# Norms with a token on each partition, a root taken ahead of the wait, and tiles that start at whole lines

## The reference, cut to what matters

```
def rmsnorm(x, g):
    xf = x.astype(jnp.float32)
    y = xf * lax.rsqrt(jnp.mean(xf * xf, axis=-1, keepdims=True) + NORM_EPS)
    return (y * g.astype(jnp.float32)).astype(x.dtype)
...
h = rmsnorm(x, norm_mlp_g[i])
x = x + jnp.square(jax.nn.relu(h @ mlp_w1[i].astype(dt))) @ mlp_w2[i].astype(dt)
```

## Time and profile before

| | |
|---|---|
| median of 3 runs | 3005.48 us |
| profiled execution | 3006.16 us |
| its span | 3004.8 us |
| mean granted clock of PE | 0.946 |
| PE busy | 2687.6 us, 89% |
| PEld busy | 2184.9 us, 73% |
| DVE busy | 1499.9 us, 50% |
| ACT busy | 948.8 us, 32% |
| POOL busy | 173.7 us, 6% |
| DMA, mean over the span | 88 GB/s |

### The profile page before, as it was taken

One profiled execution on the slowest core, in us unless ns is written; L12 is line 12 of the kernel. 1 busy time (PEld: TensorE's weight loads), 2 busy tenths in 40 slices (PEclk: granted clock), 3 DMA queues, 4 the chain that ended last, 5 costly groups with the idle time before them and its releaser, 6 DMA issues.

```text
span 3004.8 us, 33501 instructions
## 1 busy us (share of the span) xinstructions
PE 2687.6 (89%) x14472; PEld 2184.9 (73%) x14472; DVE 1499.9 (50%) x1836; ACT 948.8 (32%) x1379; POOL 173.7 (6%) x185
## 2 busy tenths in 40 slices
PE   5988899979999788999968976678999989899998
PEld 4877778778878567887757953347888878688886
DVE  5654544254465247677555257655333354443334
ACT  4322223253334332222232245543222232232222
POOL 0001320000010010000012100000000000100001
PEclk9999999999999889999989998779999999999999
DMA  3210001212324034677322200002222222222221
GB/s 115 78 56 29 16 16 57 99 56 71 110 100 140 28 112 154 218 268 258 125 77 70 69 16 0 1 28 76 95 95 98 85 93 91 83 98 98 97 87 70
DMA packets 39300, 265.69 MB, mean 88 GB/s; under 512 B 4256, under 2 KB 4640, under 8 KB 8944
## 3 DMA queue, kind: packets, MB, share of 16 engines
q1 hardware_dynamic: 29520, 205.67, 19.6%
q0 software_dynamic: 8256, 55.41, 5.3%
q10 hardware_dynamic: 1376, 2.47, 0.2%
HBM read 261.43 MB, written 2.10 MB: 88 GB/s over the span
## 4 chain that ended last, share of the span: by engine, by line
PE 76%; DVE 15%; ACT 7%; issue 1%; POOL 0%; DMA 0%; DVEq 0%; ACTq 0%
PE bank L142 75%; DVE da_stat L162 1%; DVE w_lo L151 1%; DVE ada_acc L159 1%; ACT w_hi L148 1%; ACT tmp L148 1%; ACT da_p L148 1%; DVE rstd L165 1%; DVE tmp L165 1%; DVE tmp L159 1%; DVE tmp L151 1%; ACT L148 1%; PE bank L145 1%; DVE dd L151 1%; DVE v_t L159 1%
## 5 line engine op out<-in xcount | busy, mean ns | idle before, releaser
L142 PE MATMUL bank<-h_hi,w_hi 128*128 128x512 f32 (+1 forms) x2056 | 832.2, 405 | 47.9 <-DVE h_lo L159 27.2
L142 PE MATMUL bank<-h_lo,w_hi 128*128 128x512 f32 (+1 forms) x2056 | 813.9, 396 | 0.0
L142 PE MATMUL bank<-h_hi,w_lo 128*128 128x512 f32 (+1 forms) x2056 | 813.0, 395 | 0.0
L151 DVE TENSOR_TENSOR w_lo<-w_raw,w_hi 128x2048 fp32r<-128x2048 f32 (+2 forms) x197 | 445.2, 2260 | 347.3 <-ACT w_hi L148 347.3
L142 PEld LDWEIGHTS bank<-h_hi,w_hi 128*128 128x128 f32 (+1 forms) x2056 | 394.6, 192 | 142.4 <-issue 53.2
L148 ACT ACTIVATE w_hi<-w_raw 128x2048 fp32r<-128x2048 f32 (+2 forms) x197 | 370.6, 1881 | 333.5 <-PE bank L142 323.3
L142 PEld LDWEIGHTS bank<-h_hi,w_lo 128*128 128x128 f32 (+1 forms) x2056 | 393.4, 191 | 85.9 <-issue 0.8
L142 PEld LDWEIGHTS bank<-h_lo,w_hi 128*128 128x128 f32 (+1 forms) x2056 | 394.8, 192 | 79.7 <-issue 2.0
L142 PE MATMUL bank<-f_hi,w_hi 128*128 128x512 f32 x672 | 267.4, 398 | 0.0
L142 PE MATMUL bank<-f_hi,w_lo 128*128 128x512 f32 x672 | 266.8, 397 | 0.0
L142 PE MATMUL bank<-f_lo,w_hi 128*128 128x512 f32 x672 | 266.8, 397 | 0.0
(11 more groups left out here) (313 smaller groups left out, 3289.2 us busy)
## 6 DMA issues: line engine op xcount, KB each, us to landing
w_raw<-in_pack_ffn SPq DMA_DIRECT2D x60, 1024.0 KB, 4.9
ada_w<-in_ada_w POOLq DMA_DIRECT2D x48, 1024.0 KB, 5.2
w_raw<-in_pack_mlp SPq DMA_DIRECT2D x32, 1024.0 KB, 6.8
w_raw<-in_pack_gdn_qkv SPq DMA_DIRECT2D x12, 1024.0 KB, 4.9
w_raw<-in_pack_sc_cu SPq DMA_DIRECT2D x8, 1024.0 KB, 4.9
w_raw<-in_pack_ffn SPq DMA_DIRECT2D x8, 768.0 KB, 4.3
w_raw<-in_pack_gdn_z SPq DMA_DIRECT2D x4, 1024.0 KB, 4.9
w_raw<-in_pack_gate_a SPq DMA_DIRECT2D x4, 1024.0 KB, 4.9
```

What stands on the lines that cost most here:

```text
L142: return self.engine.matmul(*a, **k) if self.engine is not None else self
L151: return self.engine.tensor_tensor(*a) if self.engine is not None else self
```

## The change

Norms:
- `over_partitions` makes four matmuls of one column (two for 256 tokens): the sum's slice of 128 tokens is the stationary operand, one column of ones the moving one. The result has a token on each partition and one column for each slice of 128 tokens.
- `root` first takes the root of the column eps into `spare_col`, then waits, then takes the root of these four (two) columns into `stat_cols`. `inverse` takes their reciprocals.
- A new `spread` on PE waits for these, and makes four (two) fp32 matmuls of 128 columns: the stationary operand is one column of `stat_cols` broadcast over 128 columns, the moving one the identity. This puts each token's factor on every partition, in a bank of the `work` ring. `scale` (and the final scalings of `end` and `fin`) read it there and free the bank with the last tile.
- PE issues `spread` directly behind `over_partitions`. In mem and ctx one `yield` is put between the two, and one more `yield` each on ACT's and DVE's lanes ahead of the norm's tiles.

Layout: `prm` is padded to 384 columns and `sil` to 128, `mod`, `lam_col`, `lam_pr`, the norms' columns and the spare one lie in one tile `small` of 128 columns, and `gated_inverse` lies in `sq0`. Tiles' starts before and after, by the sum of sizes in bytes past a multiple of 512: `x_t`, `h_*`, `w_*` 128 and 128; `kept_consts`, `mod` 480 and 128; `rstd` 416 and 128; `tmp`, `sq`, memory, context and attention tiles 448 and 128; `o_hi`, `o_lo` 64 and 128; `f_hi`, `f_lo` 32 and 128; `ada_w` 0 and 128.

```diff
@@ -263,17 +263,20 @@
 
 
     W4 = [P, 4, P]
+    whole_lines = lambda columns: -(-columns // P) * P
     x_t = sb(top, "x_t", [P, DT, T])
     h_hi = sb(top, "h_hi", [P, DT, T], F32R)
     h_lo = sb(top, "h_lo", [P, DT, T], F32R)
     w_raw = [sb(top, f"w_raw{i}", [P, DT * PW]) for i in range(2)]
     w_hi = [sb(top, f"w_hi{i}", [P, DT * PW], F32R) for i in range(2)]
     w_lo = [sb(top, f"w_lo{i}", [P, DT * PW], F32R) for i in range(2)]
-    prm = sb(top, "prm", [P, N_PARAMS])
+    prm = sb(top, "prm", [P, whole_lines(N_PARAMS)])[:, 0:N_PARAMS]
     kept_consts = sb(top, "kept_consts", [P, N_KEPT, P])
-    mod = sb(top, "mod", [P, 112])
+    small = sb(top, "small", [P, P])
+    mod, lam_col, stat_cols = small[:, 0:112], small[:, 112:116], small[:, 116:120]
+    lam_pr = small[0:64, 120:122]
+    spare_col = small[:, 124:125]
     rstd = sb(top, "rstd", [P, T])
-    lam_col = sb(top, "lam_col", [P, 4])
     tmp = [sb(top, f"tmp{i}", [P, T]) for i in range(4)]
     sq = [sb(top, f"sq{i}", [P, T]) for i in range(2)]
     banks = [top.enter_context(nc.psum_tensor(f"bank{i}", [P, 512], F32)) for i in range(8)]
@@ -281,7 +284,7 @@
 
     mix = ExitStack()
     gate_rows = sb(mix, "gate_rows", [32, T])
-    gated_inv = sb(mix, "gated_inverse", [P, 8 * NCH])
+    gated_inv = sq[0][:, 0:8 * NCH]
     o_t = sb(mix, "heads_t", [P, DT, T])
     q_t, z_t = o_t, x_t
     with ExitStack() as st:
@@ -339,11 +342,10 @@
         x_stat = [sb(st, f"xstat{i}", [P, 12]) for i in range(2)]
 
     with ExitStack() as st:
-        sil = sb(st, "sil", [P, 16])
+        sil = sb(st, "sil", [P, whole_lines(16)])[:, 0:16]
         ada_w = [sb(st, f"ada_w{i}", [P, 2, 1024]) for i in range(3)]
         ada_acc = [sb(st, f"ada_acc{i}", [P, 1024]) for i in range(2)]
         ada_accc = sb(st, "ada_accc", [P, 1024])
-        lam_pr = sb(st, "lam_pr", [64, 2])
         f_hi = sb(st, "f_hi", [P, 8, T], F32R)
         f_lo = sb(st, "f_lo", [P, 8, T], F32R)
 
@@ -579,20 +581,40 @@
                 V.tensor_tensor(self.out, self.out, self.room(k), ALU.add).then_inc(*up("dve_sum", (self.name, k)))
 
         def over_partitions(self, T_, rings):
+
             bank, before = rings.stat.take(("stat", self.name))
             T_.wait_ge(*freed(before))
             T_.wait_ge(*self.added(self.n - 1))
-            T_.matmul(bank[:, 0:self.tokens], const("ones"), self.out, start=True, stop=True).then_inc(
-                *up("pe_stat", self.name))
+            for c in range(self.tokens // P):
+                done = T_.matmul(bank[:, c:c + 1], self.out[:, c * P:(c + 1) * P], const("ones")[:, 0:1], start=True,
+                                 stop=True)
+            done.then_inc(*up("pe_stat", self.name))
+
+        def spread(self, T_, rings):
+            bank, before = rings.work.take(("spread", self.name))
+            T_.wait_ge(*freed(before))
+            T_.wait_ge(*at("dve_rstd", self.name))
+            for c in range(self.tokens // P):
+                done = T_.matmul(bank[:, c * P:(c + 1) * P], stat_cols[:, c:c + 1].to_broadcast([P, P]),
+                                 const("ident"), start=True, stop=True)
+            done.then_inc(*up("pe_stat", ("spread", self.name)))
 
         def root(self, S):
+
+            n = self.tokens // P
+            S.activation(spare_col, param("eps"), ACT.Sqrt)
             S.wait_ge(*at("pe_stat", self.name))
-            S.activation(self.out, bank_of(("stat", self.name))[:, 0:self.tokens], ACT.Sqrt, bias=param("eps"),
+            S.activation(stat_cols[:, 0:n], bank_of(("stat", self.name))[:, 0:n], ACT.Sqrt, bias=param("eps"),
                          scale=1.0 / (self.n * P)).then_inc(*up("act_root", self.name, frees=("stat", self.name)))
 
         def inverse(self, V):
+            n = self.tokens // P
             V.wait_ge(*at("act_root", self.name))
-            V.reciprocal(self.out, self.out).then_inc(*up("dve_rstd", self.name))
+            V.reciprocal(stat_cols[:, 0:n], stat_cols[:, 0:n]).then_inc(*up("dve_rstd", self.name))
+
+        def rstd_of(self, lane):
+            lane.wait_ge(*at("pe_stat", ("spread", self.name)))
+            return bank_of(("spread", self.name))[:, 0:self.tokens]
 
     class Norm:
 
@@ -608,10 +630,10 @@
                 V.wait_ge(*at("dve_h_lo", (self.name, k - 4)))
             elif self.tmp_free is not None:
                 V.wait_ge(*at(*self.tmp_free))
-            V.wait_ge(*at("dve_rstd", self.name))
             V.wait_ge(*self.ready(k))
-            V.scalar_tensor_tensor(tmp[k % 4][:, 0:self.tokens], self.src(k), self.gain(k), self.total.out, ALU.mult,
-                                   ALU.mult).then_inc(*up("dve_scaled", (self.name, k)))
+            V.scalar_tensor_tensor(tmp[k % 4][:, 0:self.tokens], self.src(k), self.gain(k), self.total.rstd_of(V),
+                                   ALU.mult, ALU.mult).then_inc(
+                *up("dve_scaled", (self.name, k), frees=("spread", self.name) if k == DT - 1 else None))
 
         def round_hi(self, S, k):
             y, h = tmp[k % 4][:, 0:self.tokens], self.hi[:, k, 0:self.tokens]
@@ -1778,6 +1801,8 @@
         for _ in range(6 + DT):
             yield
         mem_sum.over_partitions(T_, rings)
+        yield
+        mem_sum.spread(T_, rings)
         for _ in range(1 + DT):
             yield
...
@@ -2119,11 +2148,11 @@
                             end_sum if blk == MLP_BLOCKS - 1 else None)
         V.finish()
         end_sum.inverse(V)
-        V.wait_ge(*at("dve_rstd", "end"))
         for k in range(DT):
             V.wait_ge(*at("dve_x", ("mlp3", k)))
-            V.scalar_tensor_tensor(x_t[:, k, :], x_t[:, k, :], param("norm_final_g", k, k + 1), rstd[:, :], ALU.mult,
-                                   ALU.mult).then_inc(*up("dve_x", ("end", k)))
+            V.scalar_tensor_tensor(x_t[:, k, :], x_t[:, k, :], param("norm_final_g", k, k + 1), end_sum.rstd_of(V),
+                                   ALU.mult, ALU.mult).then_inc(
+                *up("dve_x", ("end", k), frees=("spread", "end") if k == DT - 1 else None))
         for k in range(DT):
             da_sum.add_vector(V, k)
```

More of the change, by code:

```diff
@@ L1773, in memory_tensor @@
         xa_sum.over_partitions(T_, rings)
+        xa_sum.spread(T_, rings)
         drain(gemm_tensor(T_, rings, "xk", h_done(mem_norm), m_hi, m_lo, MEM))
@@ L2073, in mlp_tensor @@
         mlp_sum.over_partitions(T_, rings)
+        mlp_sum.spread(T_, rings)
         T_.background, T_.pace = modulation_tensor(T_, rings), 3
@@ L2079, in mlp_tensor @@
         end_sum.over_partitions(T_, rings)
+        end_sum.spread(T_, rings)
     def mlp_scalar(S):
@@ L2144, in context_tensor @@
         da_sum.over_partitions(T_, rings)
+        da_sum.spread(T_, rings)
         T_.background, T_.pace = ctx_norm_tensor(T_, rings), 4
@@ L2184, in ctx_norm_tensor @@
         ctx_sum.over_partitions(T_, rings)
+        yield
+        ctx_sum.spread(T_, rings)
         for _ in range(1 + DT):
@@ L2479, in ffn_tensor @@
         ffn_sum[layer].over_partitions(T_, rings)
+        ffn_sum[layer].spread(T_, rings)
         for blk, (k0, nk) in enumerate(FFN_BLOCKS):
@@ L2552, in short_tensor @@
         sc_sum.over_partitions(T_, rings)
+        sc_sum.spread(T_, rings)
         drain(gemm_tensor(T_, rings, "sc_cu", h_done(sc_norm)))
@@ L2626, in tensor_program @@
         mix_sum.over_partitions(T_, rings)
+        mix_sum.spread(T_, rings)
         gates_tensor(T_, rings)
@@ L2641, in tensor_program @@
         fin_sum.over_partitions(T_, rings)
+        fin_sum.spread(T_, rings)
     def scalar_program(S):
@@ L2684, in vector_program @@
         fin_sum.inverse(V)
-        V.wait_ge(*at("dve_rstd", "fin"))
         for k in range(DT):
             V.wait_ge(*at("dve_x", ("ffn1_2", k)))
-            V.scalar_tensor_tensor(x_t[:, k, :], x_t[:, k, :], param("final_g", k, k + 1), rstd[:, :], ALU.mult,
-                                   ALU.mult).then_inc(*up("dve_out", k))
+            V.scalar_tensor_tensor(x_t[:, k, :], x_t[:, k, :], param("final_g", k, k + 1), fin_sum.rstd_of(V),
+                                   ALU.mult, ALU.mult).then_inc(
+                *up("dve_out", k, frees=("spread", "fin") if k == DT - 1 else None))
     def pool_program(G):
```

## The result

The changed kernel takes 2987.03 us (median of 4, 2986.37 to 2988.07) against 3005.61 (4 runs, 3004.14 to 3007.47): a ratio of 0.9937, interval 0.9921 to 0.9953, 18.6 us less. The prediction was 2984, range 2965 to 3001. The profiled execution is 2988.07 with a span of 2986.7 and a mean granted clock of 0.944 (0.946 before).

The account below looks back on a forecast made before the run. PE was taken to bound the kernel (76% of the chain), with norms as waiting chains between; layout 16.0 plus visible norms 11.9 less 6.5 lost at mem, xa, ctx gave 21.4 off 3006.16, so 2984 us, range 2965 to 3001.

Parts of the forecast that it names:

- Pace of f and o: Matmuls on f and o, by the layout, go at h's pace of 0.2267 us: 17.8 us less before deductions.
- B: Matmuls on f and o: alignment does nothing, the memory region does; norms alone then give 3000 us; chance 0.16.
- lines and boundaries of the tile's own start: Moving operands of f and o: a line fetched across a boundary slows them, so equal alignment gives h's pace.
- I take off 1.8: In the mlp, part of the f gain is lost to waits at DVE's ada_acc additions: 17.8 becomes 16.0.
- Visible norms: Norms where PE waits (end, sc, fin, ffn1, da, ffn0, mix, mlp): shorter chains gain 11.9 us, bounds 8 and 18.
- forecast's 4.4 for a cold spread: In a visible norm, last add to first scaling: 3.45 us warm, 4.4 with a cold spread, 5.4 all cold.
- mlp: At mlp's norm the spare root moves the 1.28 us ACT table load ahead of the wait; gain 2.8 in all.
- mem, xa, ctx: Where PE went straight on into a GEMM it now waits for spread: losses 1.9, 1.5 and 3.1, sum 6.5 us.
- Norms alone: All norms together: 11.9 us gained where visible less 6.5 lost at mem, xa and ctx, net 5.4.
- Rival D: After mlp, ffn0, sc and ffn1 norms the clock stays up: 11.2 us more gained, 2973; chance 0.14.
- Rival C: At mem, xa, ctx PE's spread waits cost 9.5 against 8 gained, no layout term: 3007 us; chance 0.06.

Follow-up runs that it names:

- inert padding: The kernel before with 256 bytes of padding ahead of o_hi and 256 ahead of f_hi: 3007.23 us, ratio 0.9999.
- o and f alone with spread later: Kernel before with changed norms, padding moving only o and f to the weights' start, and spread issued later at xa, mem, ctx: 2985.31 us, ratio 0.9917.
- three norms as before: The changed kernel with the norms mem, xa and ctx in their old form and order: 2979.04 us, ratio 0.9903.
- more distances: The changed kernel with f_hi and f_lo at +32, +96, +16 and -32 from the weight panels' start in mlp, ffn0, sc, ffn1: 2995.56 us, one run.

## Why the prediction was right, and where it wasn't

The time and the sign are right, in part by luck, as the parts show:

- **Pace of f and o.** The rate was right to 0.1 ns (0.2267 for both, 17.8 us), and B, that the address does nothing, is out. The reason given, lines and boundaries of the tile's own start, is wrong: the distance to the stationary operand decides. The change hits it by luck, because it puts everything at the same start as the weights.
- **What of it reaches the end.** "I take off 1.8" is the step that failed. Alone the layout gives 4.5, not 16. The reason named for the 1.8, DVE's additions in the mlp, isn't where it went: 4.75 of 5.8 arrive there. What comes back is of two kinds.
  - First, the layout slows other tiles, to which the prediction gave nothing. With 256 columns the start to start of matmuls on m and on c is 118 ns (median) in the old layout and 120 in the new, with these tiles as moving and as stationary operand alike; where m is stationary and the weights move, three traces of the old layout (norms alone, inert padding, o and f alone with spread later) even have 113, why isn't settled. For 256 columns 0 isn't the best distance. With 192 matmuls in each of four groups this is 1.5 us.
  - Second, the granted clock: 0.942 instead of 0.946. In the one program of spread later with o and f alone, 0.001 of the clock goes with some 2.9 us (11.8 over 0.947 to 0.943). An estimate from that: brought to 0.946, layout alone is 2990.6, the norms alone 2997.3, the changed kernel 2981, so 15, 9 and 25 less; there the parts add, and 16 was near. The clocks have three digits, so each difference is good to some 2 us, and no run holds the clock fixed: that the clock takes the rest is argued, from the runs' clocks and from the low grants in the stretches that lose.
  - Why the layout's programs get a lower clock isn't settled. It is no plain effect of moving tiles (inert padding: 0.945 to 0.946), nor of less PE work as such (three norms as before: 0.947).
- **Visible norms.** Forecast 11.9. From last add to first scaling after: mix 4.73, mlp 4.01, end 4.73, da 4.82, ffn0 4.82, sc 3.81, ffn1 4.61, fin 3.48; before 6.34, 6.85, 5.38, 6.52, 6.51, 5.45, 5.79, 5.39. The sum of the differences is 13.2. The terms: spread was cold (2.09) in six of eight, where a warm 1.3 was half counted on; ones cost 1.04 to 1.85. Five of the eight chains are longer than the forecast's 4.4 for a cold spread, since ones was cold too, in whole or in part; the total is larger all the same, because mix, da and ffn0, whose ones were cold before as well, gain 1.6 to 1.7 each and not 0.9 to 1.1.
- **mlp.** 2.84 gained, 2.8 forecast, the load gone from the way; without the spare root it is back and only there.
- **mem, xa, ctx.** Forecast 6.5: 1.9, 1.5, 3.1. From mem's last add to xa's are 2.0 us more than before; from xa's to the end of the GEMMs on m 53.4 instead of 51.2, so 2.2; ctx 3.2. Together 7.4. But of the 2.0 at mem, 1.2 stand in the layout alone too. Beside three norms as before, in one layout, it is 0.9, 1.9 and 3.0, together 5.7: the total was right, mem half of its forecast. That the old form in these three is better is shown; of the 8.8 us between the two traces 5.7 lie there, and the rest elsewhere, with its clock at 0.947 beside 0.944. xa's loss isn't the wait alone: spread is cold (2.08, where 1.1 was counted) and the first panel partly at half clock (0.78 beside 1.00, 0.4 us), which the prediction had as a threat at ctx, not here.
- **Norms alone.** 9.0 less, not 5.4. In that trace the eight chains give 15.1 (end's is 3.05 there, its ones and spread warm) and the three places cost 7.0, so 8.2 of the 9.0 are found by place: what was mis-sized is the sum of visible gains, 11.9 for 15.1.
- **Rival D** (the clock stays up after the norms) is out: over the ten us after mlp, ffn0 and sc the grants are 0.68, 0.82 and 0.68 where they were 0.66, 0.74 and 0.74. The rule of the Trainium skill, "TensorE: Matmul & The Clock Gate", section "Why this matters for your kernels", would have kept it up, for PE's pauses are now short. Here two short pauses around few small matmuls were followed by grants as low as one long one before, and at xa by a lower grant where one short pause had left it at 1.00. **Rival C** is out by the sign, though its place was the right one: with 7.4 against 13.2 it stood halfway.
- The Trainium skill's rule for the spacing of warm matmuls, on the same page, section "Wait — 56ns, not 53.3ns?", gives 215.7 ns at 512 columns. No stretch here comes below 226.6, and nine distances give five paces.

So the total was right in part by luck. Alone, the layout missed by 11.5 one way and the norms by 3.6 the other, and their sum of 13.5 lies 5 short of the 18.6 measured together. That 18.6 came near the forecast 21.4 rests on these 5 as well, which the clock may explain (0.944 together, 0.942 with the layout alone) and no run shows.

## What to carry to other kernels

Read the pace of matmuls by operand, from starts over gapless stretches; when two operands of one shape differ, compare where each starts against the stationary operand's start modulo 256 bytes, and try it for each column count, since 512 and 256 wanted different distances here. A shorter chain through small matmuls belongs only where PE stood anyway; where PE went straight on, it puts a wait and a cold start into a dense stretch. And take a gain in pace to the span by way of the granted clock: a count of matmuls times nanoseconds was nearly right for bare stages (3.5, 1.3 and 3.7 us of 4.0, 1.5 and 4.0) and gave 17.8 for a whole that measured 4.5, with a lower mean clock beside it.

## What the runs showed that I had not expected

- The pace of gapless 128x512 matmuls depends on the distance between the two operands' starts: 226.7 ns at 0 and up to 234.3 elsewhere, with a jump of 5 ns for 16 bytes, and a better place at +64 (229.0).
- One program's time goes with its mean granted clock, 2975.7 at 0.947 and 2987.5 at 0.943, on one chip within minutes.
- The differential attention, from the last 256-column matmuls on h to its output GEMM, took 262.8 us before, 265.9 in the changed kernel and 268.2 with three norms as before; with o and f alone moved it was 262.7. Its 96 matmuls on da_pt show 674, 710, 737 and 676 ns (the last with the changed norms). It isn't the tiles' starts: with o and f alone and spread later those tiles had their old starts, and it was 266.0 and 711, and with more distances they had the new ones, and it was 262.7 and 673. The grants differ (0.80 and 0.81 over the stage); what sets them stays open.
